# Gated delta heads of a hybrid decoder trunk: the same pieces in another order on VectorE, ScalarE and TensorE

## What is computed

```
def gdn_mixer(qkv, z, b_raw, a_raw, ...):
    q, k, v = split(silu(causal_dwconv(qkv, conv_w)))      # width 4, per channel
    q, k, v = l2n(heads(q)), l2n(heads(k)), heads(v)       # x * rsqrt(sum x^2 + eps)
    o = gated_delta_rule(q, k, v, g, beta)
    return rmsnorm(o, norm_g) * silu(heads(z))

# gated_delta_rule, per head and chunk of 64
decay = exp(where(causal, gc_i - gc_j, -inf))
L     = strict(beta k k^T) * decay;  T = inverse(I + L)
u, w  = T (beta v),  T (beta k exp(gc));  attn = causal(q k^T) * decay
for each chunk:                                            # in order
    v_new = u - w state
    o     = (q exp(gc)) state + attn v_new
    state = state * exp(g_last) + k_dec^T v_new
```

## Time and profile before

| What | Value |
|---|---|
| Runs | 2729.97 us median of 3 (2726.71 to 2733.36) |
| Profiled execution | 2732.31 us; span of its instructions 2730.5 us |
| PE matmul busy | 2625.6 us, 96% of the span |
| PE weight load busy | 2434.1 us, 89% |
| DVE / ACT busy | 1765.6 us, 65% / 1131.3 us, 41% |
| Chain that ended last | PE 85%, DVE 8%, ACT 3% |
| Mean granted TensorE clock | 0.986 of full speed |
| One pair of heads | 112.2 us (q's convolution starts at 187.05, 299.23 and 411.27 us) |

### The profile page before, as it was taken

One profiled execution on the slowest core, in us unless ns is written; L12 is line 12 of the kernel. 1 busy time (PEld: TensorE's weight loads), 2 busy tenths in 40 slices (PEclk: granted clock), 3 DMA queues, 4 the chain that ended last, 5 costly groups with the idle time before them and its releaser, 6 DMA issues.

```text
span 2730.5 us, 46605 instructions
## 1 busy us (share of the span) xinstructions
PE 2625.6 (96%) x18448; PEld 2434.1 (89%) x18448; DVE 1765.6 (65%) x2499; ACT 1131.3 (41%) x1470; POOL 10.0 (0%) x18
## 2 busy tenths in 40 slices
PE   6898998999899999999999999999899999999999
PEld 5898898899898899889988988899788998899889
DVE  4666666665777764776477666765777647764774
ACT  2434444343444443444344344444444434443443
POOL 0000000000000000000000000000000000000000
PEclk8899999999999999999999999999999999999999
DMA  5343443345445565556555543345256655566554
GB/s 153 101 124 101 116 117 102 123 155 170 147 145 187 185 191 180 182 186 191 180 182 187 169 149 108 109 132 165 90 185 192 192 183 181 186 190 183 181 188 150
DMA packets 429635, 432.64 MB, mean 158 GB/s; under 512 B 15487, under 2 KB 427796, under 8 KB 429108
## 3 DMA queue, kind: packets, MB, share of 16 engines
q1 hardware_dynamic: 422832, 422.63, 50.3%
q0 software_dynamic: 1584, 5.40, 0.7%
q10 hardware_dynamic: 5076, 2.56, 0.3%
HBM read 428.44 MB, written 2.10 MB: 158 GB/s over the span
## 4 chain that ended last, share of the span: by engine, by line
PE 85%; DVE 8%; ACT 3%; issue 2%; DMA 1%; SPq 0%; POOL 0%; ACTq 0%; DVEq 0%
PE stream L1537 24%; PE stream L1522 13%; PE stream L1524 13%; PE stream L1523 13%; PE stream L1538 12%; PE bank L1616 1%; PE bank L1557 1%; DVE w_lo L904 1%; ACT scores L838 1%; PE bank L1506 1%; ACT w_hi L492 1%; PE stream L1616 1%; DMA cst<-in_consts 1%; DMA stage<-in_mem 1%; DVE v_buf L958 0%
## 5 line engine op out<-in xcount | busy, mean ns | idle before, releaser
L904 DVE TENSOR_TENSOR w_lo<-w_raw,w_hi 128x1024 fp32r<-128x1024 f32 x800 | 966.0, 1222 | 587.7 <-ACT w_hi L492 583.9
L492 ACT CAST w_hi<-w_raw 128x1024 fp32r<-128x1024 f32 x800 | 835.6, 1048 | 832.9 <-PE stream L1524 481.9
L1537 PE MATMUL stream<-h,w_hi 128*128 128x512 f32 x2816 | 992.2, 398 | 0.0
L1538 PE MATMUL stream<-h,w_lo 128*128 128x256 f32 x2816 | 788.9, 280 | 0.0
L1537 PEld LDWEIGHTS stream<-h,w_hi 128*128 128x128 f32 x2816 | 528.9, 188 | 130.3
L1522 PE MATMUL stream<-act,w_hi 128*128 128x256 f32 x2016 | 577.5, 286 | 1.0 <-DVE act L931 1.0
L1524 PE MATMUL stream<-act,w_lo 128*128 128x256 f32 x2016 | 570.7, 283 | 0.0
L1523 PE MATMUL stream<-act,w_hi 128*128 128x256 f32 x2016 | 570.5, 283 | 0.0
L1538 PEld LDWEIGHTS stream<-h,w_lo 128*128 128x128 f32 x2816 | 531.4, 189 | 0.1
L1522 PE MATMUL stream<-h,w_hi 128*128 128x256 f32 x1536 | 462.2, 301 | 3.1 <-DVE w_lo L904 3.1
L1523 PE MATMUL stream<-h,w_hi 128*128 128x256 f32 x1536 | 440.6, 287 | 0.0
(11 more groups left out here) (356 smaller groups left out, 1728.0 us busy)
## 6 DMA issues: line engine op xcount, KB each, us to landing
w_raw<-in_ffn_in_w SPq DMA_DIRECT2D x352, 512.0 KB, 4.5
w_raw<-in_ffn_out_w SPq DMA_DIRECT2D x176, 512.0 KB, 3.9
w_raw<-in_hyb_in_w SPq DMA_DIRECT2D x96, 512.0 KB, 3.9
w_raw<-in_swa_in_w SPq DMA_DIRECT2D x48, 512.0 KB, 3.6
w_raw<-in_xkv_w SPq DMA_DIRECT2D x32, 512.0 KB, 3.4
w_raw<-in_hyb_out_w SPq DMA_DIRECT2D x32, 512.0 KB, 3.5
w_raw<-in_swa_out_w SPq DMA_DIRECT2D x32, 512.0 KB, 3.5
w_raw<-in_xq_w SPq DMA_DIRECT2D x16, 512.0 KB, 3.6
```

Source lines behind the costliest of these rows:

```text
L492: nc.scalar.copy(whi[:, k], raw[:, n % NRAW]).then_inc(hi_split, 1)
L904: v.tensor_tensor(wlo[:, k], raw[:, n % NRAW], whi[:, k].bitcast(F32), ALU.subtract).then_inc(lo_split, 1)
L1537: mm(bank[:, m, :], whi[:, k, kk, w], h[:, kt, :, :], start=(q == 0 and kk == 0), stop=False, skip_group_check=True)
L1538: last = mm(bank[:, m, 0:TOK], wlo[:, k, kk, w], h[:, kt, 0, :], start=False, stop=(q == 3 and kk == len(kts) - 1), skip_group_check=True)
```

## The change

No arithmetic is added or removed. On DVE and ACT the tail of the pair before now goes ahead of the front within each tick, so that in tick 3 DVE updates the state and ends the LRU before it starts q's evacuation and convolution, and in ticks 7 and 8 ACT does the output's square and norm before k's SiLU and the squares of q and k. PE's order of front and tail stays. DVE's `hyb_front(p, 12)` (LT and attnT) goes ahead of the low split of that tick, waits for the decay's exp alone, and gives `lt_ready` after LT; q_dec follows after a wait of its own; the two level-1 masks of LT that lay in tick 13 now follow it in tick 12. In ticks 9 to 11 keys come ahead of queries: sums, Ln, Exp, multiply, each with a semaphore of its own, and PE makes k k^T and the transposes of k before it waits for q. The broadcast of gates moves from the end of tick 10 to tick 9.

```diff
@@ ACT gdn_front
                 if t == 9:
-                    act.wait_ge(qk_ss, p + 1)
+                    act.wait_ge(qk_ss, 2 * p + 1)
                     tables(LN_EXP)
-                    f(W4[:, 2, :], B[0][:], ACT.Ln, bias=eps_col)
-                    link(f(W4[:, 3, :], B[1][:], ACT.Ln, bias=eps_col))
+                    f(W4[:, 3, :], B[1][:], ACT.Ln, bias=eps_col)
+                    act.wait_ge(qk_ss, 2 * p + 2)
+                    link(f(W4[:, 2, :], B[0][:], ACT.Ln, bias=eps_col))
+                    f(W4[:, 3, :], W4[:, 3, :], ACT.Exp, scale=-0.5).then_inc(qk_r, 1)
                     f(W4[:, 2, :], W4[:, 2, :], ACT.Exp, scale=-0.5, bias=lnq_col).then_inc(qk_r, 1)
-                    f(W4[:, 3, :], W4[:, 3, :], ACT.Exp, scale=-0.5).then_inc(qk_r, 1)
@@ ACT loop over pairs and ticks
                     split(HYB + PAIR_TICKS * p + t + AHEAD)
-                    gdn_front(p, t)
                     if p:
                         gdn_tail(p - 1, t)
-                    else:
+                    gdn_front(p, t)
+                    if not p:
                         gates(t)
@@ DVE hyb_front
-                    dve.wait_ge(qk_n, p + 1)
+                    dve.wait_ge(qk_n, 2 * p + 2)
...
-                if t == 10:
-                    dve.wait_ge(qk_r, 2 * p + 2)
+                if t == 9:
                     if p:
                         dve.wait_ge(os_done, 4 * p)
                         dve.wait_ge(uw_done, p)
-                    v.tensor_tensor(qb[:], qb[:], W4[:, 2, :], ALU.mult)
-                    v.tensor_tensor(kb[:], kb[:], W4[:, 3, :], ALU.mult)
                     for hh in range(2):
                         for buf, src in ((kbe, gg), (kdec, beta)):
                             s = c3(src)[:, :, 2 * p + hh:2 * p + hh + 1].to_broadcast([P, TT, P])
-                            last = v.tensor_copy(buf[:, hh * TOK:hh * TOK + TOK].rearrange("p (t m) -> p t m", t=TT), s)
-                    last.then_inc(qk_n, 1)
+                            v.tensor_copy(buf[:, hh * TOK:hh * TOK + TOK].rearrange("p (t m) -> p t m", t=TT), s)
+                if t == 10:
+                    dve.wait_ge(qk_r, 2 * p + 1)
+                    v.tensor_tensor(kb[:], kb[:], W4[:, 3, :], ALU.mult).then_inc(qk_n, 1)
+                    dve.wait_ge(qk_r, 2 * p + 2)
+                    v.tensor_tensor(qb[:], qb[:], W4[:, 2, :], ALU.mult).then_inc(qk_n, 1)
                 if t == 12:
-                    dve.wait_ge(dexp, 3 * p + 3)
+                    dve.wait_ge(dexp, 3 * p + 1)
                     v.tensor_tensor(LT[:], B[2][:], W4[:, 3, :], ALU.mult)
                     link(v.tensor_tensor(at[:], B[3][:], W4[:, 3, :], ALU.mult))
-                    v.tensor_tensor(LT[:], LT[:], B[4][:], ALU.mult)
+                    v.tensor_tensor(LT[:], LT[:], B[4][:], ALU.mult).then_inc(lt_ready, 1)
                     v.tensor_tensor(r4(at[:]), r4(at[:]), c_("tri").unsqueeze(1).to_broadcast([P, 4, P]), ALU.mult)
-                    v.tensor_tensor(qd[:], qb[:], vb[:], ALU.mult).then_inc(lt_ready, 1)
+                    dve.wait_ge(dexp, 3 * p + 3)
+                    link(v.tensor_tensor(qd[:], qb[:], vb[:], ALU.mult))
+                    link(v.tensor_tensor(r4(W4[:, 2, :]), r4(LT[:]), mask("level1T"), ALU.mult))
+                    v.tensor_tensor(r4(W4[:, 2, :]), mask("ident"), r4(W4[:, 2, :]), ALU.subtract)
                 if t == 13:
                     dve.wait_ge(lx_done, 6 * p + 1)
-                    v.tensor_tensor(r4(W4[:, 0, :]), r4(B[2][:]), mask("level1"), ALU.mult)
-                    link(v.tensor_tensor(r4(W4[:, 2, :]), r4(LT[:]), mask("level1T"), ALU.mult))
-                    v.tensor_tensor(r4(W4[:, 1, :]), mask("ident"), r4(W4[:, 0, :]), ALU.subtract)
-                    v.tensor_tensor(r4(W4[:, 2, :]), mask("ident"), r4(W4[:, 2, :]), ALU.subtract).then_inc(tu_ready, 1)
+                    link(v.tensor_tensor(r4(W4[:, 0, :]), r4(B[2][:]), mask("level1"), ALU.mult))
+                    v.tensor_tensor(r4(W4[:, 1, :]), mask("ident"), r4(W4[:, 0, :]), ALU.subtract).then_inc(tu_ready, 1)
@@ DVE loop over pairs and ticks
+                    if t == 12:
+                        hyb_front(p, t)
                     split(HYB + PAIR_TICKS * p + t + AHEAD)
-                    hyb_front(p, t)
                     if p:
                         hyb_tail(p - 1, t)
-                    else:
+                    if t != 12:
+                        hyb_front(p, t)
+                    if p == 0:
                         gates(t)
@@ PE hyb_front
                 if t == 9:
                     pe.wait_ge(qk_sq, 2 * p + 2)
-                    mm(B[0][:], ones, W4[:, 0, :], start=True, stop=True)
                     mm(B[1][:], ones, W4[:, 1, :], start=True, stop=True).then_inc(qk_ss, 1)
+                    mm(B[0][:], ones, W4[:, 0, :], start=True, stop=True).then_inc(qk_ss, 1)
                 if t == 11:
-                    pe.wait_ge(qk_n, p + 1)
+                    pe.wait_ge(qk_n, 2 * p + 1)
                     units(B[2], kb, kb)
-                    units(B[3], kb, qb)
                     for u in range(4):
                         transpose(B[0][:, u * P:u * P + P], kb[:, u * P:u * P + P])
+                    pe.wait_ge(qk_n, 2 * p + 2)
+                    units(B[3], kb, qb)
```

More of the change, by code:

```diff
@@ L324, in trunk @@
         conv_done, silu_done = sem("conv_done"), sem("silu_done")
-        qk_sq, qk_ss, qk_r, qk_n = sem("qk_squared"), sem("qk_sumsq"), sem("qk_rstd"), sem("qk_normed")
+        qk_sq, qk_ss, qk_r, qk_n = sem("qk_squared"), sem("qk_sumsq"), sem("qk_rstd"), sem("k_q_normed")
         gram_done, dmin, dexp, lt_ready = sem("gram_done"), sem("decay_arg"), sem("decay_exp"), sem("LT_ready")
@@ L613, in gdn_front @@
                     act.wait_ge(vT_done, p + 1)
-                    act.wait_ge(lt_ready, p + 1)
+                    act.wait_ge(tu_ready, 6 * p + 1)
                     for u in range(4):
@@ L1038, in gates @@
                     link(v.tensor_tensor(bexp, cols[:, 4, :], beta, ALU.mult))
+            r4 = lambda ap: ap.rearrange("p (u i) -> p u i", u=4)
+            mask = lambda name: c_(name).unsqueeze(1).to_broadcast([P, 4, P])
             def hyb_front(p, t):
@@ L1064, in hyb_front @@
                 if t == 12:
-                    dve.wait_ge(dexp, 3 * p + 3)
-                    r4 = lambda ap: ap.rearrange("p (u i) -> p u i", u=4)
+                    dve.wait_ge(dexp, 3 * p + 1)
                     v.tensor_tensor(LT[:], B[2][:], W4[:, 3, :], ALU.mult)
                     link(v.tensor_tensor(at[:], B[3][:], W4[:, 3, :], ALU.mult))
-                    v.tensor_tensor(LT[:], LT[:], B[4][:], ALU.mult)
+                    v.tensor_tensor(LT[:], LT[:], B[4][:], ALU.mult).then_inc(lt_ready, 1)
@@ L1070, in hyb_front @@
                     v.tensor_tensor(r4(at[:]), r4(at[:]), c_("tri").unsqueeze(1).to_broadcast([P, 4, P]), ALU.mult)
-                    v.tensor_tensor(qd[:], qb[:], vb[:], ALU.mult).then_inc(lt_ready, 1)
-                r4 = lambda ap: ap.rearrange("p (u i) -> p u i", u=4)
-                mask = lambda name: c_(name).unsqueeze(1).to_broadcast([P, 4, P])
+                    dve.wait_ge(dexp, 3 * p + 3)
+                    link(v.tensor_tensor(qd[:], qb[:], vb[:], ALU.mult))
+                    link(v.tensor_tensor(r4(W4[:, 2, :]), r4(LT[:]), mask("level1T"), ALU.mult))
```

## The result

The changed kernel takes 2740.76 us (median of 9 runs, 2735.3 to 2746.8), the one before 2733.36 in the same comparison (9 runs, 2726.71 to 2740.14). The ratio is 1.0027, 95% interval 1.0015 to 1.0039: 7.4 us slower.

What follows compares the result with a forecast made beforehand. PE, busy 96% of the span, was taken to bound the kernel, so only its waits and slow clock count. Waits -2.4, clock falls +4.2 and +1.6 gave +3.4 us: forecast 2734 us, range 2727 to 2741.

Steps and rivals of the forecast that it cites:

- rival 3: Slower by clock falls in tick 5 (three pairs) and tick 15 (four): +5.6 us, with tick 9 +10.4; chance 0.30.
- the clock's term: Falls of PE's granted clock: +4.2 us after tick 5 in three pairs, +1.6 for one more in tick 15.
- the walk: Pair 2 followed in the new order with the profile's times, carrying how far PE stands behind or ahead of before.
- Walk's waits: PE's waits gone and new, summed: 3 x -0.3 us in pairs 1 to 3, -1.3 and -0.2 in pair 0; together -2.4.
- The waits: Pairs 1 to 3: new PE waits of 3.1 us (tick 5), 1.4 (9), 1.1 (14), 2.2 (15); none in 4, 8, 11, 13.
- The mechanism of tick 5: q's late SiLU delays ACT's cast, that DVE's low split, that v_new; PE waits 3.1 us where there was none.
- The hidden things: Delays claimed to cost PE no wait: piece 11's load, 2.3 us later; piece 15's low split; q's multiply, 0.6 behind.
- the fall of tick 13: Clock fall after tick 13's 2.0 us wait: claimed to cost nothing, tick 15's chain being late anyway; its going wins nothing.
- the sign "112.2 us plus 1.6 for each fall, within 0.3": Expected in the profile after: pairs 1 to 3 have a period within 0.3 us of 112.2 plus 1.6 per clock fall.
- the pair's own -0.3 that the walk carried: PE's net shift after tick 15 in each of pairs 1 to 3 from waits alone: 0.3 us ahead of before.
- The sentence of the Trainium skill on repeated short idles: Repeated short idles between matmul groups suffice to make the clock swing; by it tick 9 would fall too, 4.8 us more.
- The price of a table switch: ACT, tick 8: load plus drain about 2.66 us would lengthen tick 9's wait by 1.36 in three pairs; 1.30 was used.

## Why the prediction was right, and where it was off

The measured 2740.76 lies in the range by 0.24 us only. Of the 6.8 us above the forecast 2734, 3.4 come from the kernel before: three runs gave 2730.0 for it, nine gave 2733.4. Most of the rest is the step: +7.4 us (by the interval 4 to 11) where +3.4 was forecast. The case that came is rival 3 (chance 0.30), slower by the clock with falls in tick 5 of all three pairs and in tick 15 of all four, not the likeliest one. The direction and the mechanism were right; the size of the clock's term wasn't.

The traced pairs can be cut at four of PE's waits and sums, and each piece held against its terms of the walk (from tick 5 to tick 9, for example, -1.15 + 1.4 in each of three pairs). These rows and those shown above are the cuts of pairs 1 and 2, first before, then after:

```profile
193.89 0.33 PE L1699 MATMUL stream<-q_dec,state 128*128 128x64 f32 x2
211.80 1.02 PE L1622 MATMUL bank<-gdn_work,cst 128*128 128x512 f32 x2
...
195.79 0.43 PE L1706 MATMUL stream<-q_dec,state 128*128 128x64 f32 x2 [2.97 <-DVE v_new L1149]
215.60 1.13 PE L1628 MATMUL bank<-gdn_work,cst 128*128 128x512 f32 x2 [1.51 <-ACT gdn_work L590]
360.81 1.38 PE L1622 MATMUL bank<-gdn_work 128*128 128x128 f32 x8 [2.14 <-DVE gdn_work L1101]
```

| Piece | Before, us | After, us | Difference, all pairs | Walk's waits | Left for the clock | Clock forecast |
|---|---|---|---|---|---|---|
| tick 20 to tick 5 of the next pair | 39.0 | 41.0 | +5.9 | +5.85 | 0 | 0 |
| tick 5 to tick 9, pairs 1 to 3 | 17.91 | 19.81, 21.15, 21.04 | +8.3 | +0.75 | +7.5 | +4.2 |
| tick 9 to tick 15, pairs 1 to 3 | 31.4 to 31.6 | 28.9 | -7.65 | -7.35 | -0.3 | 0 |
| tick 9 to tick 15, pair 0 | 33.3 | 30.5 | -2.8 | -1.5 | -1.3 | 0 |
| tick 15 to tick 20, four pairs | 23.7 or 25.3 | 25.3 | +3.1 | 0 | +3.1 | +1.6 |
| Sum | 396.5 | 403.3 | +6.8 | -2.25 (rounded in the walk to -2.4) | +9.0 | +5.8 |

*The waits* were right one by one: tick 5 at 2.97 (walked 3.1), tick 9 at 1.5 (1.4), tick 14 at 1.1 (1.1), v's transposes at 0.6 (0.9), tick 15 at 2.14 (2.2), none in ticks 4, 8, 11, 13. Their terms are right too: where the clock doesn't enter, the pieces differ by what the walk carried, 5.9 for 5.85 and 7.65 for 7.35. The mechanism of tick 5 is shown, not only read: moving q's SiLU on another engine took 1.7 us off a wait that DVE and PE alone seemed to make. The hidden things stayed hidden: no wait for piece 11's load, piece 15's split or q's multiply. That the fall of tick 13 cost nothing is shown as well: with ScalarE's order alone changed it is missing in pairs 1 and 2, and from tick 13 to tick 15 are 11.13 us without it and 11.12 with it in pair 0. This is also why the waits' term is negative although PE's idle time between the same two points rose from 29.5 to 33.0 us: four low stretches went with tick 13's wait.

*The clock* was the mis-sized term. For tick 5 I took one fall in each pair, 4.2 us with 4.8 as the upper bound; five stretches came, 3.4 us in pair 1 and 6.8 in pairs 2 and 3, and they cost 7.5. A first stretch cost 1.65 (pair 1), a second one straight behind it 1.2 to 1.35 more. The bound was too low because I counted a wait once, though a second stretch can follow the first. For tick 15 I took one fall more than before and two more came, +3.1 for 1.6. The other way went luck: before, the clock was low for 6.8 us around pair 0's sums of squares, after for 3.4, which is the -1.3 of pair 0.

Waits and low clock together leave little room for a third cause. Between pair 0's sums of squares and pair 3's LRU gates the fourteen traces are from 364 to 410 us long; less PE's waits and half of the time at the lower clock, every one of them is between 352.6 and 355.3. A spread of 46 us shrinks to 2.7.

Two smaller readings were off. The 1.9 us given for the wait of tick 15 before is that of pairs 0, 2 and 3; in pair 1 it was 2.04, the longest of the four, and no fall followed it. And the sign "112.2 us plus 1.6 for each fall, within 0.3" missed: from tick 5 to tick 5 are 114.95 us with two stretches and 116.30 with three, 0.4 and 0.7 under it. In both, 0.3 is the pair's own -0.3 that the walk carried; in the second the rest is the cheaper second stretch.

The sentence of the Trainium skill on repeated short idles (TensorE: Matmul & The Clock Gate, A second HAM failure mode) had stood for a fall in tick 9 as well. The trace doesn't bear this out for that tick: no low stretch follows any of the 1.5 us waits. It fits better that waits as short as 1.25 us were followed by falls, as the last section shows; whether their repetition is what does it, no run here shows. The price of a table switch that the Trainium skill gives (ScalarE: Activation LUTs, What ACT_TABLE_LOAD costs), 2.66 us with the drain, isn't what tick 8 shows: load to next activation was 1.30 us again, the load starts as the cast ahead of it ends, and the wait of tick 9 has the size that 1.30 gives.

## What to carry over

Before a step is put first on its engine, follow the step that it displaces to the other engines: here a convolution late by 3 us held a SiLU, the SiLU a cast, the cast a split, and the split stood ahead of the result that was to come early. Work that only fills a buffer three ticks ahead belongs behind the step that an engine waits for now; one such swap in tick 14 won 12 us, where no critical step put first by itself won more than 4. Where a wait of a few microseconds recurs, put the slow clock behind it into the sum as a term of its own, and allow for more than one stretch. And ask what a fall costs where it lies: ahead of a chain that is late anyway it cost nothing, in front of PE-bound pieces 1.6 us.

## What the runs showed of the hardware

The length of a wait doesn't tell whether the clock falls. A wait of 2.0 us in tick 13 was followed by a low clock in four pairs of four before, yet with the keys' steps alone in one of four, and with ScalarE's order changed alone in pairs 0 and 3 only. There the clock is 1.00 after the same wait in pairs 1 and 2 and low in pair 3:

```profile
232.50:236.50 4.00, 3.52 (x28) 3.32 (x28) 3.96 (x7) 0.23 (x1) 0.00 (x0) 1.00 0.40 104
345.00:349.00 4.00, 3.54 (x29) 3.33 (x29) 3.97 (x7) 0.20 (x1) 0.00 (x0) 1.00 0.39 107
457.00:461.50 4.50, 3.71 (x19) 3.72 (x20) 4.40 (x8) 0.66 (x1) 0.00 (x0) 0.62 0.47 136
```

The other way round, a wait of 1.25 us in tick 5 was followed by a low clock in two pairs of three, with the small products of the state recurrence before and behind it, where waits of 1.5 us behind a full piece, in tick 9, were not in any of the four kernels that have them. What decides between such cases stays open. That falls come and go at the same place may be why executions of one kernel differ by 13 us (the one before) here; it was not tested apart. Steps of under 4 us had to be read from the traces of the pairs.
